# Even halves: plain attention before selected attention, with the selection's rounds of maxima moved into the plain attention's steps on VectorE

## The reference

```python
aq, ak, av, bq, bk, bv, iq, ik, iw, cq, ck, cg, cv, cgate = mixer_inputs(rmsnorm(xp, norm1[l]), w_in[l], pos_p, lower[l])
oa = diff_attn_prompt(aq, ak, av, lam)          # A: 6 heads, difference of two softmaxes
ob = dsa_prompt(bq, iq, iw, bk, bv, ik)         # B: 5 heads, each query sees its best 256 keys
sc, oc = hgrn2_prompt(cq, ck, cg, cv)           # C: 5 heads, gated recurrence
...
score = jnp.einsum('bqh,bqhs->bqs', wi.astype(F32), jax.nn.relu(dots))
score = jnp.where(mask, score, NEG_BIG)
_, sel = lax.top_k(score, n_sel)
```

## Time and profile before

| | us |
|---|---|
| median of 3 runs | 3888.84 |
| lowest and highest | 3884.03, 3899.14 |
| the profiled execution, its time | 3897.18 |
| its span, first to last instruction | 3895.3 |
| TensorE busy in it | 3691.7 |
| VectorE busy in it | 2065.7 |
| ScalarE busy in it | 1263.7 |

### The profile page before, as it was taken

The page is one execution under the profiler, slowest core; times in us unless marked ns, Lnnn a source line. Parts: engine busy times, 40 slices in busy tenths (PEclk is TensorE's granted clock), DMA queues, the critical chain, the costliest instruction groups (busy, mean ns, idle before and its releaser), DMA issues. The chain is left out here.

```text
span 3895.3 us, 54785 instructions
## 1 busy us (share of the span) xinstructions
PE 3691.7 (95%) x21676; PEld 2940.2 (75%) x21676; DVE 2065.7 (53%) x4711; ACT 1263.7 (32%) x2918; POOL 761.1 (20%) x812
## 2 busy tenths in 40 slices
PE   7997799999999999999999999999999999999998
PEld 5775577678777777778867777787777787788887
DVE  1674564376635554428846555067644654553442
ACT  1124333245243432222244333145344433312221
POOL 2200211111010133202000013323001011453334
PEclk9998898999999999999999999999999999999999
DMA  4332222322121223233231222335112122342223
GB/s 146 97 109 65 77 87 78 103 95 92 56 84 36 78 89 96 80 113 124 72 101 48 82 68 88 107 114 162 55 48 87 30 84 65 96 141 87 67 84 94
DMA packets 151608, 339.55 MB, mean 87 GB/s; under 512 B 30312, under 2 KB 68648, under 8 KB 138040
## 3 DMA queue, kind: packets, MB, share of 16 engines
q1 hardware_dynamic: 151352, 336.04, 27.7%
HBM read 299.31 MB, written 36.68 MB: 86 GB/s over the span
## 5 line engine op out<-in xcount | busy, mean ns | idle before, releaser
L1042 PE MATMUL PS<-xn,wring 128*128 128x272 f32 (+1 forms) x7168 | 1693.7, 396 | 24.9 <-DVE xn L1598 15.1
L1042 PEld LDWEIGHTS PS<-xn,wring 128*128 128x128 f32 x7168 | 1381.1, 195 | 288.6 <-issue 35.3
L2010 POOL TENSOR_TENSOR xT<-xT,res 128x272 f32<-128x272 f32 (+1 forms) x320 | 255.6, 800 | 2251.3 <-ACT res L1325 2211.4
L1042 PE MATMUL PS<-dense,wring 128*128 128x256 f32 (+1 forms) x2816 | 654.6, 390 | 10.4 <-ACT res L1325 5.1
L1042 PEld LDWEIGHTS PS<-dense,wring 128*128 128x128 f32 x2816 | 532.1, 192 | 106.7 <-issue 10.3
L1325 ACT ACTIVATE res<-PS 128x272 f32<-128x272 f32 (+1 forms) x320 | 123.6, 388 | 539.5 <-PE PS L1042 514.0
L1063 PE MATMUL PS<-wring,xn 128*128 128x256 f32 (+1 forms) x1152 | 266.3, 392 | 2.3 <-ACT dense L1339 2.3
L1063 PEld LDWEIGHTS PS<-wring,xn 128*128 128x128 f32 (+1 forms) x1152 | 214.4, 188 | 49.5 <-issue 5.9
L1042 PE MATMUL PS<-catT,wring 128*128 128x272 f32 (+1 forms) x1024 | 235.5, 391 | 4.7 <-issue 2.7
L1333 ACT ACTIVATE dense<-PS 128x256 f32<-128x256 f32 (+1 forms) x176 | 68.3, 389 | 521.7 <-PE PS L1042 480.9
L1042 PEld LDWEIGHTS PS<-catT,wring 128*128 128x128 f32 x1024 | 195.2, 192 | 44.8 <-issue 11.3
(11 more groups left out here) (243 smaller groups left out, 4492.7 us busy)
## 6 DMA issues: line engine op xcount, KB each, us to landing
wring<-in_wu SPq DMA_DIRECT2D x88, 1024.0 KB, 4.9
wring<-in_wf SPq DMA_DIRECT2D x88, 512.0 KB, 3.7
wring<-in_wo SPq DMA_DIRECT2D x64, 512.0 KB, 3.6
wring<-in_wd SPq DMA_DIRECT2D x96, 320.0 KB, 2.9
wring<-in_wd SPq DMA_DIRECT2D x64, 384.0 KB, 3.1
wring<-in_wn SPq DMA_DIRECT2D x16, 1024.0 KB, 5.5
kv<-out_projT SPq DMA_DIRECT2D x48, 256.0 KB, 4.2
out_projT<-dense SPq DMA_DIRECT2D x40, 272.0 KB
```

Of the source, the lines that this page charges most:

```text
L1042: mm = nc.tensor.matmul(PS[:, dbank(t.g0), 0:cw], wtile(t.q, i), rhs, start=(kk == a), stop=(kk == b - 1))
L2010: nc.gpsimd.tensor_tensor(x, x, res[:, i % NRES, 0:cw], ALU.add).then_inc(s_res, 1)
```

## The change

In half 0 the attention goes through group a first and group b second; in half 1 the order stays. Group b's bias, which the selection makes, is then needed only after the 30 items of a. So the rounds leave the X steps and stand in VectorE's part of the attention steps: three rounds (`EACH_STEP`) after the maxima and the combining of each item, in items 1 to 27. They now work in place in `bias`. X keeps 8 of its 49 steps. `step_times` adds 3.75 us of VectorE to each of the first 28 attention steps. The numbers of matmuls, vector instructions of each kind and DMAs stay as they are.

```diff
+ORDER = ("ab", "ba")
+def kv_slot(h, g, pair):
+    return pair + 3 * ORDER[h].index(g)
 def _items(h):
     out = []
-    for g in "ba":
+    for g in ORDER[h]:
...
 def _pick_steps(h):
     out = [("load", 0, 0), ("dots", 0, 0)]
+    for y in range(len(PICKS[h])):
+        out += [("near", y, 0), ("far", y, 0)]
     if h == 1:
...
-    for y, r in enumerate(ROUNDS[h]):
-        out += [("near", y, 0), ("far", y, 0)]
-        n = -(-r // BURST)
-        out += [("pick", y, z) for z in range(n)]
     return out
+EACH_STEP = 3
+ALL_ROUNDS = [(y, r) for y, n in enumerate(ROUNDS[0]) for r in range(n)]
-ATT_LOAD = [("pick", len(PICKS[0]) - 1, 2), ("bit", BITS // 2, 0)]
+ATT_LOAD = [("far", len(PICKS[0]) - 1, 0), ("bit", BITS // 2, 0)]
...
+            if h == 0 and len(out) - 1 <= len(ALL_ROUNDS) // EACH_STEP:
+                out[-1] = (*out[-1][:2], out[-1][2] + EACH_STEP * 1.25, 0)
...
-                    first = max(first, section_end(m, "b") + LAG)
+                    first = max(first, section_end(m, ORDER[h][0]) + LAG)
...
+                    if s and "a" in [it.g for it in items[max(0, s - 4):s]]:
+                        pe.wait_ge(s_ex, M0[m][next(i for i, it in enumerate(items) if it.g == "b")])
...
-                elif what == "pick":
-                    wk = work[:u.w, 0:u.nk]
-                    for r in range(BURST * z, min(BURST * z + BURST, ROUNDS[h][y])):
-                        step(nc.vector.max(top[:u.w, :], wk))
-                        step(nc.vector.match_replace(wk, top[:u.w, :], wk, SENTINEL))
...
+            def picks(s):
+                for y, r in ALL_ROUNDS[EACH_STEP * s:EACH_STEP * s + EACH_STEP]:
+                    u = PICKS[0][y]
+                    wk = bias[:u.w, u.bias:u.bias + u.nk]
+                    step(nc.vector.max(top[:u.w, :], wk))
+                    step(nc.vector.match_replace(wk, top[:u.w, :], wk, SENTINEL))
+                    if r == ROUNDS[0][y] - 1:
+                        nc.vector.tensor_scalar(wk, wk, SENTINEL, 8 * NEG, ALU.not_equal, ALU.mult).then_inc(x_bias, 1)
...
                 if 1 <= s < len(items) + 1:
                     combine(s - 1)
+                if m % 2 == 0:
+                    picks(s)
```

More of the change, by code:

```diff
@@ L325, in _pick_steps @@
     out = [("load", 0, 0), ("dots", 0, 0)]
+    for y in range(len(PICKS[h])):
+        out += [("near", y, 0), ("far", y, 0)]
     if h == 1:
-        for y in range(len(PICKS[h])):
-            out += [("near", y, 0), ("far", y, 0)]
-        return out + [("sign", 0, 0)] + [("bit", b, 0) for b in range(BITS)] + [("last", y, 0) for y in range(len(PICKS[h]))]
-    for y, r in enumerate(ROUNDS[h]):
-        out += [("near", y, 0), ("far", y, 0)]
-        n = -(-r // BURST)
-        out += [("pick", y, z) for z in range(n)]
-    return out
+        out += [("sign", 0, 0)] + [("bit", b, 0) for b in range(BITS)] + [("last", y, 0) for y in range(len(PICKS[h]))]
+    return out
+EACH_STEP = 3
+ALL_ROUNDS = [(y, r) for y, n in enumerate(ROUNDS[0]) for r in range(n)]
 PICK_STEPS = [_pick_steps(h) for h in range(2)]
-ATT_LOAD = [("pick", len(PICKS[0]) - 1, 2), ("bit", BITS // 2, 0)]
+ATT_LOAD = [("far", len(PICKS[0]) - 1, 0), ("bit", BITS // 2, 0)]
 IX_LOADS = [7 + len(PICKS[0]), 5 + len(PICKS[1])]
@@ L387, in step_times @@
                 out.append((0, 0, 10 * k, 0))
-            elif what == "pick":
-                out.append((0, 0, min(BURST, ROUNDS[h][y] - BURST * z) * 2.6 * (1.04 * k + 0.15), 0))
             else:
@@ L417, in step_groups @@
     firsts = sorted({it.first for it in items})
-    out = ["b"]
+    order = ORDER[m % 2] + "c"
+    out = [order[0]]
     for s in range(len(items) + 3):
@@ L421, in step_groups @@
         if s - 3 in firsts and s > 3:
-            g = max(g, "bac"[(firsts.index(s - 3) + 1) // 3], key="bac".index)
+            g = max(g, order[(firsts.index(s - 3) + 1) // 3], key="bac".index)
         out.append(g)
@@ L782, in load_pair @@
             jj = 9 * m + j
-            g, pair = "bac"[j // 3], j % 3
+            g, pair = (ORDER[h] + "c")[j // 3], j % 3
             pw = P if 2 * pair + 1 < HEADS[g] else D
@@ L790, in load_pair @@
             elif jj >= 2:
-                sp.wait_ge(s_pv, I0[user] + len([it for it in ITEMS[user] if it.pair + (3 if it.g == "a" else 0) <= uj]))
+                sp.wait_ge(s_pv, I0[user] + len([it for it in ITEMS[user] if kv_slot(user % 2, it.g, it.pair) <= uj]))
             rq, rk, cv = {"a": (R_AQ, R_AK, C_AV), "b": (R_BQ, R_BK, C_BV), "c": (R_CQ, R_CF, C_CI)}[g]
@@ L1094, in idx_tensor @@
                     dots(y, 1)
-                elif what == ("far" if h == 1 else "pick") and z == (0 if h == 1 else 6) and y + 1 < len(PICKS[h]):
+                elif what == "far" and y + 1 < len(PICKS[h]):
                     dots(y + 1, 0)
@@ L1104, in scores @@
                 g, pair, hh, u, first, last = items[s]
-                j = m * 9 + pair + (3 if g == "a" else 0)
+                j = m * 9 + kv_slot(m % 2, g, pair)
                 pe.wait_ge(s_kv[j % 2], kv_loaded(m, j % 9))
@@ L1164, in values @@
                 g, pair, hh, u, first, last = items[s]
-                v = v_of(m * 9 + pair + (3 if g == "a" else 0))
+                v = v_of(m * 9 + kv_slot(m % 2, g, pair))
                 if not last:
@@ L1686, in idx_vector @@
                 if what in ("near", "far"):
-                    wk = kept(u) if h == 1 else work[:u.w, 0:u.nk]
+                    wk = kept(u)
                     for hh in range(2):
@@ L1693, in idx_vector @@
                             dve.wait_ge(x_in, 16 * sum(IX_LOADS[i % 2] for i in range(m + 1)))
-                            dve.wait_ge(x_bias, sum(len(PICKS[i % 2]) for i in range(m)) + (y if h == 0 else 0))
+                            dve.wait_ge(x_bias, sum(len(PICKS[i % 2]) for i in range(m)))
                             nc.vector.tensor_scalar(wk, rl[:u.w, hh, 0:u.nk], iw[:u.w, u.slot, 0:1], None, ALU.mult).then_inc(x_acc, 1)
@@ L1702, in idx_vector @@
                             step(nc.vector.memset(wk[0:64, u.nk - 64:u.nk], NEG))
-                elif what == "pick":
-                    wk = work[:u.w, 0:u.nk]
-                    for r in range(BURST * z, min(BURST * z + BURST, ROUNDS[h][y])):
-                        step(nc.vector.max(top[:u.w, :], wk))
-                        step(nc.vector.match_replace(wk, top[:u.w, :], wk, SENTINEL))
-                    if BURST * z + BURST >= ROUNDS[h][y]:
-                        nc.vector.tensor_scalar(bias[:u.w, u.bias:u.bias + u.nk], wk, SENTINEL, 8 * NEG, ALU.not_equal, ALU.mult)\
-                            .then_inc(x_bias, 1)
                 elif what == "sign":
```

## The result

The changed kernel takes 3949.65 us (median of 4 runs, 3948.40 to 3959.57) against 3889.62 before (4 runs): ratio 1.0161, 95% interval 1.0143 to 1.0178. It is 60 us slower. I had said 24 slower by the profile, 3913 with a range up to 3945: right side, too small by more than half.

A forecast was written before the change was run, and what follows sets the result against it. TensorE was taken to bound the kernel, busy 3691.7 of 3895.3 us. Pass 0's stages summed to 756 against 740, +16, and pass 2 added +8: +24 in all, 3921 on the profile, 3913 against the median, range 3884 to 3945.

The forecast's parts named there:

- Attention a in pass 0: Stage a of pass 0: VectorE becomes the bound, 232 us replacing 184, bounds 228 and 250.
- lockstep: Attention a: TensorE's and VectorE's steps add up instead of overlapping; the sum allowed no more than 4 us of waiting.
- The sign that I had named: Attention a: VectorE idle for over 20 us would make the forecast wrong towards slower.
- third rival: Much slower: engines in lockstep, a 250 us in pass 0, 25 more in pass 2, C 205; +74, 3963; chance 0.10.
- C in pass 0: C of pass 0 loses 8 turns to a and shrinks from 216 to 190 us, bounds 185 and 205.
- Attention b: Attention b in pass 0 keeps its 9 turns, 25 items and chain: 88 us, bounds 80 and 92.
- The start: Before a in pass 0: 5 us for bunched indexer products, 7.5 us idle while the first scores wait for loads.
- Pass 2: Attention a of pass 2: TensorE stays the bound, VectorE 94% busy beside it; +8 us, bounds -6 and +25.
- no change: Whole kernel: C at 185 and the start's 5 us hidden make +14, level pass 2 makes +6, 3895; chance 0.35.
- Faster: Pass 0's b and C: the lower clock goes away, winning 31 us; total -7, 3882; chance 0.13.
- The clock stays low: All of a in pass 0 at 1.2 GHz: TensorE's 177 us become 354, total 4035; chance 0.02.
- The rounds were not slowed beside GpSimd: Attention a: rounds beside GpSimd's rotations, 30.9 us busy there, keep their speed; if slowed, the stage would only grow.

The follow-up runs named there:

- rounds_between: Changed kernel with first loads of a allowed one turn behind their section, and each step's three rounds between maxima and combination; 3960.69 us, ratio 1.0182 to the kernel before.
- no_rounds_p0: Changed kernel with pass 0's 81 pairs of maximum and replacement left out; 3919.18 us, ratio 1.0067 to the kernel before.
- pass2_only: Pass 2 as in the changed kernel, pass 0 as in the kernel before; 3905.37 us, ratio 1.0033 to the kernel before.
- some_woven: Kernel before with pass 0 changed: a first, early loads, 17 rounds woven one to a step, 64 kept ahead of the attention; ratio 0.9985.

## Why the prediction was wrong

The side was right, but four terms were too small, and they all erred to one side. In pass 0 the sum and the trace part by +4 us at the start, +12 in a, -4 in b and +9 in C: an end at 777 instead of 756.

**Attention a in pass 0: 232 predicted, 244 measured.** This is the step that failed: "VectorE becomes the bound of this stage", costed as VectorE's work end to end plus 4 us, with its waits for TensorE at nothing. The work was not the error: 206 us busy, less than the 107 and 110 that I added up. What was wrong is that this chain would let VectorE work without a break. It was idle 38 us where the sum had 15 (11 of gaps and 4 at the norms), and VectorE's waits in the stage say on whom (102.4 of the first row lie ahead of it):

```profile
DVE PS L1787 <- PE PS L1144: 112.1, 5, 102.4
DVE scr L1797 <- PE PS L1171: 6.1, 1, 6.1
DVE mx L1789 <- PE PS L1144: 3.8, 1, 3.8
DVE inv L1602 <- ACT inv L1331: 3.8, 1, 3.8
```

The first three, 9.7 + 6.1 + 3.8, are 20 us for TensorE's scores and transposes; the norms took the 4 that I gave them. With 81 rounds VectorE reached 84 to 88% in every kernel, whether with 26 turns (226 us) or 39 (237 to 253). I dismissed the lockstep by "TensorE may run ahead of VectorE by about the three rounds"; rounds_between shows that TensorE's transposes sit right behind the combination. The sign that I had named came, "a VectorE idle for over 20 us in a towards slower". My third rival had a at 250, pass 2 at +25 and a total of 3963, and came nearer (3950) than my forecast did; it had 0.10.

One item of the changed stage on VectorE, in order of time: the end of a step's rounds, the first of its two maxima, the combination of the item before, and the next rounds:

```profile
262.17 0.54 DVE L1775 MATCH_REPLACE8 bias<-top,bias 128x384 f32<-128x384 f32 x1
...
262.94 0.42 DVE L1789 TENSOR_REDUCE mx<-PS 128x1 f32<-128x256 f32 x1
...
264.93 0.35 DVE L1815 SCALAR_TENSOR_TENSOR scr<-scr,rs 128x128 f32<-128x128 f32 x1
265.20 0.55 DVE L1774 MAX8 top<-bias 128x8 f32<-128x384 f32 x1
```

In this step VectorE has no break, as I had costed all of them; over the stage it has its 38 us all the same. VectorE's groups of the stage say what the rounds are (busy us, mean ns | idle), beside the earlier trace rows:

```profile
L1774 DVE MAX8 top<-bias 128x8 f32<-128x384 f32 (+2 forms) x81 | 52.0, 643 | 1.8
L1775 DVE MATCH_REPLACE8 bias<-top,bias 128x384 f32<-128x384 f32 (+2 forms) x81 | 50.8, 627 | 0.0
```

**C in pass 0: 190 predicted, 199 measured, and 5 less to gain.** I set C's loss of 8 turns against 216 us and an end at 740. By turn 136's start the end was 734.4, so C was 210 and gave back 11 us, where I booked 26. Bounds 185 to 205 held it. The clock was 0.89 (0.91 before), and the idle time rose from 17.6 to 27.3 us. I let 8 turns go at their full price; no_rounds_p0 shows the same idle time without rounds, so it goes with the missing turns and not with the rounds. Attention b took 84 us for the 88 of the sum.

**The start: 5 and 7.5 us predicted, 7.0 and 9.4 measured.** The wait for the loads is as I described it, 2 us longer: the last load was issued at 244.33 and the scores began at 250.12, 5.8 us later, where I had 4.0. Early loads won 13 to 20 us in the end for 10 at the place, which I did not price; the intervals leave the 10 possible. Of the 7.0 us by turn 54, 5.3 were there at turn 20, in code that is the same; seventeen profiles have that turn between 89.6 and 95.5 us. The bunched products then cost some 2 us, so my 5, near the 7.0, was right by luck.

**Pass 2: +8 predicted, +21 by the profiles and +13 by the median of pass2_only**, within the bounds (-6 to +25). The mechanism was wrong, and that the bounds held it was luck. I expected the woven rounds to make TensorE wait; leaving them out saves nothing measurable. What costs is the order, which I took as free, through C's clock at least in part, and by the profiles the plan, through TensorE's idle time in C (22 us after 13).

**The base.** I summed against one profile whose pass 0 took 630 us, where three others of the same pass took 614 to 620. Against the mean of all four the change costs pass 0 some 47 us, not 38. I took the profile's 8.3 us over the median off the total; by these profiles they lay in the pass that I was costing.

The rivals: *no change* needed C at 185 and got 199. *Faster* needed a better clock in b and C; it was 0.88 and 0.89 after 0.86 and 0.91. *The clock stays low* did not happen, 0.88 in a. The Trainium skill (TensorE: Matmul & The Clock Gate, What's actually happening) calls the lower clock the default that activity lifts. Here the stage had neither of the two levels throughout: 0.88 on the mean means 1.2 GHz for about a quarter of it.

The rounds were not slowed beside GpSimd: in a, with 31 us of GpSimd's work, the two passes of a round took 643 and 627 ns, and 646 and 627 before. In the kernel before, the replacement over 384 keys took 542 ns on the mean both in the 24 cases with a GpSimd instruction beside it and in the 40 without. That agrees with the rule of the Trainium skill (SBUF — State Buffer, Who interferes with whom) for VectorE instructions with one SBUF input.

## What to carry to other kernels

Work that is free beside a fully busy TensorE is not free inside a chain of short steps, even if that chain's engine is busy only 58% of the time. Here 49 rounds at two to a step, with VectorE 81% busy, cost nothing that could be measured, and 81 at three to a step, at 87%, cost 33 us more; which of the two, the fill or the length of what stands in one step, ends the free room was not separated. Fill such a stage in part and leave the rest where it was; and put the filling behind what the next engine waits for, not ahead of it (28 us here, in two passes). Turns that are moved to cover the filling are missed where they were: C kept 10 us more of idle time in pass 0, with or without rounds. When a section is moved to the front, look at what its first step needs by then (10 us at the place), and when stage lengths are compared, take several profiles of the unchanged pass first: one had 630 us where the others had 614 to 620.

## What was unexpected of the hardware

The granted clock of a stage went with what stands ahead of it: 1974 products in C of pass 2 took 218.0 us at 0.98 with the plain half ahead of them, and 224.2 at 0.95 with the selected half. One profile of seven with the plain half ahead had 0.95 too (some_woven), so it is a tendency and not a rule. And code that no edit touches starts its turn 20 anywhere from 89.6 to 95.5 us in seventeen profiles.
